# First half of the input loaded as two quarters, with the order of the first turns and products changed to match

## What is computed

```
h = concatenate([meta, x])                          # 16 + 512 rows of 1024
h = layer_norm(alpha * h + 0.5 * swiglu(h, w_gate, w_up, w_down))       # ffn 1, D_FF = 2816
h = layer_norm(alpha * h + hybrid_mixer(h, ...))    # sparse attention and mLSTM head groups
h = layer_norm(alpha * h + 0.5 * swiglu(h, ...))    # ffn 2
return h[16:]

def swiglu(x, w_gate, w_up, w_down):
    return (jax.nn.silu(x @ w_gate) * (x @ w_up)) @ w_down
```

## Time and profile before

| | us |
|---|---|
| median of 3 runs | 1091.86 |
| lowest, highest | 1090.96, 1093.9 |
| the profiled execution | 1091.33 |
| its span | 1089.6 |
| mean granted TensorE clock | 0.995 |

### The profile page before, as it was taken

One profiled execution on the slowest core, in us unless ns is written; L12 is line 12 of the kernel. 1 busy time (PEld: TensorE's weight loads), 2 busy tenths in 40 slices (PEclk: granted clock), 3 DMA queues, 4 the chain that ended last, 5 costly groups with the idle time before them and its releaser, 6 DMA issues.

```text
span 1089.6 us, 16097 instructions
## 1 busy us (share of the span) xinstructions
PE 1065.8 (98%) x6619; PEld 928.1 (85%) x6619; DVE 460.0 (42%) x748; ACT 343.0 (31%) x456; POOL 110.5 (10%) x87
## 2 busy tenths in 40 slices
PE   8999999999999999999998999999999999999995
PEld 7999999999999998689875568878888888888885
DVE  5332332332322344689876533652323333222326
ACT  4322322322211235544327532552323232222121
POOL 2000000000111134012413004310000000000000
PEclk9999999999999999999999999999999999999998
DMA  6433233232223233122210002234242333153222
GB/s 196 117 89 104 77 88 104 77 93 64 81 81 105 81 99 116 39 79 78 78 39 21 19 1 62 55 85 109 77 115 77 104 89 88 50 153 92 82 77 77
DMA packets 159184, 90.39 MB, mean 83 GB/s; under 512 B 6612, under 2 KB 156808, under 8 KB 159144
## 3 DMA queue, kind: packets, MB, share of 16 engines
q1 hardware_dynamic: 159144, 89.83, 29.0%
HBM read 87.72 MB, written 2.10 MB: 82 GB/s over the span
## 4 chain that ended last, share of the span: by engine, by line
PE 92%; DVE 4%; ACT 3%; issue 1%; DMA 0%; DVEq 0%; SPq 0%
PE ps L943 75%; PE ps L1171 4%; PE ps L1453 2%; PE ps L1433 1%; PE ps L1444 1%; ACT xh L729 1%; ACT x L730 1%; PE ps L1461 1%; PE ps L1237 1%; DVE wlo L1528 1%; PE ps L1084 0%; PE ps L1086 0%; PE ps L1085 0%; DMA xin<-in_x 0%; DVE ps L1719 0%
## 5 line engine op out<-in xcount | busy, mean ns | idle before, releaser
L943 PE MATMUL ps<-xh,whi 128*128 128x264 f32 (+1 forms) x1256 | 353.6, 331 | 2.8 <-ACT xh L729 1.9
L943 PE MATMUL ps<-xh,wlo 128*128 128x264 f32 (+1 forms) x1256 | 349.8, 329 | 0.0
L943 PE MATMUL ps<-xl,whi 128*128 128x264 f32 (+1 forms) x1256 | 345.5, 328 | 0.7 <-DVE xl L1545 0.7
L943 PEld LDWEIGHTS ps<-xh,whi 128*128 128x128 f32 x1256 | 210.7, 189 | 32.0 <-issue 5.6
L943 PEld LDWEIGHTS ps<-xh,wlo 128*128 128x128 f32 x1256 | 212.3, 189 | 21.3 <-issue 0.2
L943 PEld LDWEIGHTS ps<-xl,whi 128*128 128x128 f32 x1256 | 211.4, 189 | 22.3 <-DVE xl L1545 0.9
L1528 DVE TENSOR_TENSOR wlo<-wraw,whi 128x2048 fp32r<-128x2048 f32 (+1 forms) x81 | 168.5, 2080 | 138.2 <-ACT whi L632 138.2
L632 ACT ACTIVATE whi<-wraw 128x2048 fp32r<-128x2048 f32 (+1 forms) x89 | 152.5, 1713 | 131.3 <-PE ps L943 125.4
L1584 DVE TENSOR_TENSOR ht<-ps,sil 128x528 f32<-128x528 f32 (+1 forms) x44 | 30.8, 700 | 249.0 <-PE ps L943 248.0
L943 PE MATMUL ps<-hh,whi 128*128 128x264 f32 (+1 forms) x462 | 123.8, 322 | 0.0
L943 PE MATMUL ps<-hl,whi 128*128 128x264 f32 (+1 forms) x462 | 123.5, 321 | 0.0
(11 more groups left out here) (247 smaller groups left out, 951.1 us busy)
## 6 DMA issues: line engine op xcount, KB each, us to landing
wraw<-in_ffn_w_gate SPq DMA_DIRECT2D x43, 512.0 KB, 4.0
wraw<-in_ffn_w_up SPq DMA_DIRECT2D x43, 512.0 KB, 5.2
wraw<-in_ffn_w_down SPq DMA_DIRECT2D x32, 384.0 KB, 3.4
wraw<-in_ffn_w_down SPq DMA_DIRECT2D x32, 320.0 KB, 3.9
wraw<-in_w_in SPq DMA_DIRECT2D x19, 512.0 KB, 4.4
wraw<-in_w_out SPq DMA_DIRECT2D x8, 512.0 KB, 4.5
xin<-in_x SPq DMA_DIRECT2D x2, 1024.0 KB, 6.5
out<-zrow SPq DMA_DIRECT2D x8, 256.0 KB, 2.0
```

Source lines behind the costliest of these rows:

```text
L943: mm = pe.matmul(ps[:, b + e, 0:width], w, mov, start=(first and n == 0), stop=(last and n == 2))
```

## The change

- The input comes in three loads of whole k tiles, `X_TILES = (0, 2, 4, 8)`: tiles 0 and 1, tiles 2 and 3, tiles 4 to 7. The meta tokens come in one load of their own, first, with their own semaphore `meta_in`.
- The gate's first part is loaded between the two quarters, the up matrix's first part between the second quarter and the second half.
- `WARM_START` is 6 instead of 10.
- TensorE turns tiles 0 and 1, makes the gate's passes 0 and 1 for them, and turns 2 and 3 behind that; turn 4 comes behind the up products of tiles 0 and 1, and turn 5 behind those of tiles 2 and 3, right ahead of turn 6.
- On VectorE `first_low(1)` comes ahead of `x_low(2)`.

```
-WARM_START, WARM_NORM = 10, 20
+WARM_START, WARM_NORM = 6, 20
+X_TILES = (0, 2, 4, 8)
...
-                w = slice(c * (D // 2), (c + 1) * (D // 2))
-                sp.dma_start(xin[0:N_META, 0, w], a["meta_tokens"][:, w]).then_inc(rows_in[c], 16)
+                w = slice(X_TILES[c] * P, X_TILES[c + 1] * P)
                 sp.dma_start(xin[:, 1:NT, w], a["x"][0].rearrange("(j p) d -> p j d", p=P)[:, :, w]).then_inc(rows_in[c], 16)
...
+                    sp.dma_start(xin[0:N_META, 0, :], a["meta_tokens"][:, :]).then_inc(meta_in, 16)
                     load_inputs(0)
-                    for m, w in enumerate((g, v)):
-                        sp.dma_start(dst[:, m, 0:4], w[:, 0:4, bass.ts(f, P)]).then_inc(first_in[m], 16)
+                    sp.dma_start(dst[:, 0, 0:4], g[:, 0:4, bass.ts(f, P)]).then_inc(first_in[0], 16)
                     load_inputs(1)
+                    sp.dma_start(dst[:, 1, 0:4], v[:, 0:4, bass.ts(f, P)]).then_inc(first_in[1], 16)
+                    load_inputs(2)
...
-                if k % 4 == 0:
-                    pe.wait_ge(rows_in[k // 4], 16 * 2)
+                if k == 0:
+                    pe.wait_ge(meta_in, 16)
+                if k in X_TILES:
+                    pe.wait_ge(rows_in[X_TILES.index(k)], 16)
...
-                    for k in range(4):
-                        turn(k)
+                    turn(0)
+                    turn(1)
                     pe.wait_ge(first_lo, 1)
-                    first_unit(range(4), (0,), ((0, 1),))
-                    first_unit(range(4), (0,), ((2,),))
-                    turn(4)
+                    first_unit((0, 1), (0,), ((0, 1),))
+                    turn(2)
+                    turn(3)
+                    first_unit((0, 1), (0,), ((2,),))
+                    first_unit((2, 3), (0,), ((0, 1),))
                     pe.wait_ge(first_lo, 2)
                     first_unit((0, 1), (1,))
+                    first_unit((2, 3), (0,), ((2,),))
+                    turn(4)
+                    first_unit((2, 3), (1,))
                     turn(5)
-                    first_unit((2, 3), (1,))
                     turn(6)
                     pe.wait_ge(w_lo, 1)
                     first_unit((4,), (0, 1))
...
                 copy_in(3)
+                first_low(1)
                 x_low(2)
-                first_low(1)
                 x_low(3)
```

More of the change, by code:

```diff
@@ L234, in build @@
         const_ready = sem("const_ready")
-        rows_in = [sem(f"rows_in{c}") for c in range(2)]
+        meta_in = sem("meta_in")
+        rows_in = [sem(f"rows_in{c}") for c in range(3)]
         vrows_in = sem("vrows_in")
```

## The result

| | before | changed |
|---|---|---|
| median of 20 runs, us | 1091.82 | 1096.22 |
| lowest, highest | 1090.04, 1094.76 | 1092.3, 1098.36 |
| ratio, 95% interval | | 1.0034 [1.0025, 1.0043] |
| the profiled execution, its span | 1091.33, 1089.6 | 1094.73, 1093.0 |

The account below looks back on a forecast made before the run. TensorE bounds the kernel, so a prologue shift reaches the end: start 1.3 us earlier, 0.5 lost to the clock, waits near 4 against 1.7, net 1.3 later; 1091.6 plus that gives 1092.9 us, range 1090.2 to 1095.4.

Parts of the forecast that it names:

- What bounds the kernel, and where the change can act: TensorE, 98% busy; the change acts only in the prologue ahead of 26.38 us, and a shift there reaches the end unchanged.
- F: Start of the first product of k tile 4, 19.33 us before; forecast 20.6, 1.3 later.
- The loads: Input loads at the start: the first quarter of x there at 5.3 us, a gain of 1.3.
- The second quarter: Load of x tiles 2 and 3, forecast to land at about 7.6 us, before it is asked for.
- The three waits: TensorE's idle time in the new prologue, counted as 1.6, 0.55, 0.3 and 1.5 us, near 4.
- F' = M' + 11.75: New first product of tile 4 comes 11.75 us behind the new first real product; before, the distance was 9.69.
- the wait behind turn 6: TensorE idles 1.5 us ahead of tile 4's first product, until VectorE's low part of the upper k tiles is done.
- the one for the clock: First turns after the shorter warm-up: the clock rises at 6.4 us, a microsecond at half speed, 0.5 us lost.
- M: Start of the first real product on TensorE, 9.64 us before; forecast 8.85.
- the race: Rival, chance 0.17: GpSimd's xl 0 goes ahead of VectorE's gate low part, up to 1.3 us more; 1094.2 us.
- the low clock: Rival, chance 0.07: prologue stays at 1.2 GHz, 5 us over forecast, 1097.9; 1095.1 if rising only behind about 16 us.
- that pause: TensorE idle from the end of turn 1 to the first real product, some 1.6 us.

Follow-up runs that it names:

- e1: The changed kernel with WARM_START back at 10; median 1096.2 us, ratio to the kernel before 1.0029.
- e3: The changed kernel with turn 5 moved right behind turn 4, ahead of the up products of tiles 2 and 3; median 1094.9 us, ratio 1.0023 to before.
- e2: The kernel before with WARM_START 6 instead of 10 alone; median 1091.7 us, ratio to the kernel before 0.9998.
- e5: The kernel before, with its loads and ten warm-up products, and only the changed order on TensorE and VectorE; median 1096.0 us, ratio 1.0038 to before.
- e9: The changed kernel with six unread products of mean_w between turn 1 and the wait for the gate's low part; median 1093.9 us, ratio 1.0013 to before.
- e8: The changed kernel with WARM_START 10, turn 5 right behind turn 4, and six unread products behind turn 1; median 1092.3 us, ratio 1.0005 to before.
- e10: The changed kernel with GpSimd's first xl made to wait for the gate's low part; median 1095.2 us, ratio 1.0034 to before.
- e4: The changed kernel with WARM_START 10 and turn 5 moved right behind turn 4; median 1094.1 us, ratio 1.0015 to before.
- e7: The changed kernel with the old order of TensorE and VectorE, WARM_START still 6; median 1092.3 us, ratio 1.0006 to before.
- e6: The changed kernel with the old order of TensorE and VectorE and WARM_START 10; median 1092.8 us, ratio 1.0004 to before.

## Why the prediction was wrong

- *What bounds the kernel, and where the change can act*: right. The whole shift stands at unit 1, and 7.05 us lie from F to unit 1 in both kernels (24.04 to 31.09). That the part behind it has one length was wrong: it varies by 3 us between profiles, with the clock near 490 and 588 us.
- *The loads*: the quarter's landing was right (first turn 5.55 against 5.34 forecast). The second quarter was an error, 8.7 to 8.9 instead of 7.6, without effect in the new order, where turn 2 comes at 12.38.
- *The three waits and F' = M' + 11.75*: right at full clock, 11.95 in e1; the wait behind turn 6 (1.5 forecast, 1.25 measured) is confirmed by e3.
- *The term that failed is the one for the clock*, "if the clock again rises at 6.4, and the first turns run a microsecond at half speed: 0.5 us lost". It took one time from one trace, in which TensorE had not stopped, and used it for a kernel in which it stops twice. In the profile of the changed kernel the clock was low until about 14.5: through turns 0 and 1, the first eight products and turns 2 and 3. Against the forecast M was 1.5 late (0.2 landing, some 0.5 for the turns at half speed and their late copies, 0.75 for the gate's low part behind GpSimd) and M to F 2.0 longer (13.72 against 11.75, and 11.95 at full clock in e1), 3.4 together.
- *The rivals*: the race, at 0.17, was there in the profile; the low clock, at 0.07, named the right mechanism with far too small a chance. Its price for a clock that rises only behind about 16 us, 1095.1, is near the profiled 1094.73; its seven turns were priced low (2.5 us for them, where a turn took 1.26 instead of 0.75, so some 3.6). It blamed the short warm-up and the idle stretch together. e1 and e2 show that the warm-up alone is not it, e5 that the order is, and e9, with e8, that filling the pause the order opens ahead of M gives back about 2 us. The prediction had counted that pause, 1.6 us, as plain idle time. I also treated the two rivals as apart, though a slow turn 1 is what loses the race.
- *The range*: 1095.4 as its upper end left out the low clock, and 13 of the 20 runs lie above it. The profiled execution, with its low clock, lies inside at 1094.73; with the longest of the parts behind unit 1 seen in the profiles, 3 us more, the same prologue would give 1097.7 (an estimate). So where a run lies in the range or above it is in part decided far behind the change.

Open is how the time divides between the low clock's two ways in, never having risen (the changed kernel, e3, e10) and falling again (e4, e5): the runs' mean clock leaves out all that lies ahead of the first change, it takes in the stretches near 490 and 588 us, and only one execution of each kernel has a profile. Open too is what decides in an execution whether the clock rises and holds: six warm-up products had it up within the first turn in e7 (two turns in 1.64 us, against 2.56), which has the loads and the start of the changed kernel, and not in the changed kernel. And open is what a closed race brings in the median.

## What to carry to other kernels

An idle stretch opened on TensorE near the start is not worth only its own length: in this kernel it could cost the clock of the next 3.4 to 6.8 us (e4, e5), and six useless products in it gave back about 2 us (e9, e8). When an order is rewritten so that work starts earlier, look at what the moved steps used to hide: turns 2 and 3 filled TensorE's time while VectorE's chain to the first product ran, and twelve products between two turns did so for another chain; a step that only feeds a later wait should have work behind it. An earlier first load gained nothing by itself (e6, e7), since the third turn then waited for the second. And one profile is one execution: the clock held through the pause in e1 and fell in e4.

## What the runs showed that I had not expected

- The clock fell behind a pause of 1.5 us that came after 5 us of work and two turns (e4), and held through the same place when it was filled (e8), but also once when it was not (e1).
- A low clock during the first four turns and the first products (e2) cost nothing in the median: 1091.73 against 1091.77. A fall at turn 2 in the old order (e6, e7) moved F by no more than 0.4 us.
- The kernel before has this spread too: of its 30 runs beside e5, the 14 with a mean clock of 0.995 average 1090.5 us, the 11 with 0.991 to 0.993 average 1094.1. Much of what looks like noise of the measurement goes with the clock; which stretches they were, in the prologue or near 490 and 588 us, the mean does not tell.
